# A two-layer hybrid trunk: three rounded passes for every mixer chunk, with half slots, a ring of six and remainders on GpSimd

## Chip, cores and metric

The kernel runs on one core of one Trainium2 chip. The metric is the device time of one launch in microseconds, from the first to the last instruction and what lies around them; lower is better. Engines: TensorE (PE) multiplies, VectorE (DVE), ScalarE (ACT) and GpSimd (POOL) work on tiles in SBUF, and SyncE (SP) issues the DMA of the weights.

## The reference

The input x is 256 tokens by 1024 channels, f32. There are two layers. In each:

- `h = rmsnorm(x)`, then one projection `z = h @ w_in` whose columns feed four mixers and four gates. A is a gated MLP (`u * (W_s @ layernorm(v))`), B is causal pooling with windows 2, 4, 8 and 16, C is RWKV-7 (eight heads of 64, a delta-rule state), D is Mamba-2 SSD (eight heads, a causal convolution of width 4).
- `merged = sum_k sigmoid(G_k) * (y_k @ w_branch[k])`, then `x = x + merged @ w_out`.
- `h = rmsnorm(x)`, then a dense SwiGLU (inner width 3584) in layer 0, and the best two of eight SwiGLU experts for each token in layer 1.

A last rmsnorm gives the output. Mixer C normalises `kk` by the norm of each head, and its output by the variance of each head; both are sums over 64 channels.

## The kernel before

**The stream of weights.** All large weights lie in HBM as one stream of chunks of 128 x 2048 f32 (1 MB), in the order of use: 19 chunks of the projection (NZ; `Z_UNITS` names them zg, xbc, v, u, b, c), 24 of the merge (N_MERGE: for each of 8 steps two of gates and one of a branch projection), 4 of the output, 42 of a feed-forward block, and so on; 472 in all. SP loads them into `ring`, seven slots, and reuses a slot when PE has raised `chunks_used`.

**Two kinds of matmul.** For a plain f32 matmul PE reads `ring` and `h` directly (two records in the trace for each call of `mm`). For a rounded product, `three` makes three passes: rounded weight by rounded activation, rounded by remainder, and remainder by rounded. ACT rounds the whole chunk into `w_high` (two slots, L1167 in the mixer), and DVE subtracts it from the chunk in place, which gives `ring_low` (`z_low`, L1660). Before the change this is done for the first NS = 12 chunks of a layer's mixer, for the dense FFN and for the experts; chunks 12 to 18, the merge and the output are plain f32.

**The order of work.** PE's order is written out by hand. `project` computes a layer's chunks 0 to 18; between them stand `mixer_d_rows` (after chunk 13), `mixer_d_out` (after 15), `mixer_d_norm` (after 16) and `mixer_a`, `mixer_b` (after 17). Then comes `mixer_c`, a long serial chain: LoRA matmuls, head norms, then for each of two chunks of time the scores and six levels of doubling, in which PE, DVE and ACT hand tiles to each other. Between its links PE does quarters of merge chunks as filler. `SIDE` lists how many: 12 before the LoRA matmuls ("cw"), 4 before the head sums ("ss"), 12 before the bonus ("bo"), 8 before the transposes ("kt"), one to three at each level, 4 each at "mu" and "va". The branches are merged in the order A, B, D, C, so C is needed last. `merge` does the remaining chunks and the output matmuls.

**Each engine works in program order.** ACT evacuates the projection's banks (`evacuate`), takes the sigmoids of the gates (`gates`, L1158) and the exponentials and roots of the mixers. DVE does the rest of the mixers and multiplies gates by projections (`products`). POOL makes the pooling of mixer B and adds the products of steps 2 to 7 into `mg` (L1330). For head norms PE sums the 64 channels of each head with a 128 x 128 matrix of ones and zeros, `heads`, so that the sums are spread over all channels, and DVE takes the reciprocal of 128 x 1024 numbers (L1546 for `kk`, L1618 for the output).

**Lines that the text below uses.** L1006 and L1009 are the squares and the square root of a norm on ACT; between them ACT rounds the first two chunks (`meanwhile`). L1051 is an exponential of a 128 x 1024 tile on ACT. L1492 and L1494 are mixer C's token shift on DVE: one difference of 128 x 3584 and 14 multiply-adds. L1555 makes `nb`, the last tile that PE's transposes "kt" and "nt" (L466) wait for. L1570 masks a tile out of PSUM, and L1572 adds the identity to it in SBUF. L1594 adds a level's result.

Of the kernel before, what the change touches and what calls it, by code (L numbers as in the profile page):

```python
# [28 lines left out]
RING = 7  # L48
# [9 lines left out]
NS = 12  # L58
MERGE_ORDER = [0, 1, 3, 2]
# [5 lines left out]
SIDE = [("cw", 12), ("ss", 4), ("bo", 12), ("kt", 8)]  # L65
# [4 lines left out]
SIDE += [("mu", 4), ("va", 4)]  # L70
# [16 lines left out]
for _name, _k in PP_LIST:  # L87
# [6 lines left out]
           ("off", LEVELS * P), ("count", 4 * T), ("reset", 4 * T), ("sel", H * P), ("slots", CAP), ("slot", 1)]  # L94
# [4 lines left out]
NCC = _n  # L99

SW_LIST = [("w_s", 512), ("pool", 512), ("w2a2", 512), ("g2", 512), ("dt", 64), ("router", 64)]
SW, _n = {}, 0
for _name, _k in SW_LIST:
# [11 lines left out]
for _c in range(NCH):  # L115
    _r = 2 * _c
# [9 lines left out]
    if _c == 0:  # L126
        M_USES += [("S", 2)]
M_USES += [("mu0", 1), ("mu1", 2), ("va0", 3), ("va1", 0)]
# [30 lines left out]
def trunk(nc, x_in, stream, pp_in, cc_in, sw_in, rep_in, out):  # L159
    with ExitStack() as ctx:  # L160
# [6 lines left out]
        x = sb("x", [P, DT, T])  # L167
        h = sb("h", [P, DT, T])
        ring_at = -(-nc.sbuf_base // 32) * 32
        ring = sb("ring", [P, RING, CW])  # L170
        cc = sb("cc", [P, NCC])
        pp = sb("pp", [P, L, NPP])
        sw = sb("sw", [P, NSW])
        rep = sb("rep", [P, NREP])
        rstd = sb("rstd", [P, T])
        rms = sb("rms", [P, T])
        small = sb("small", [P, 256])
        arena_at = -(-nc.sbuf_base // 32) * 32
        arena = sb("arena", [P, 28264])
# [68 lines left out]
        wb = area(24168, 512)  # L248
        ub = area(24680, 512)
# [5 lines left out]
        oo = tiles(12840, 4)  # L255
# [3 lines left out]
        k2 = tiles(24168, 4)  # L259
# [3 lines left out]
        sg = area(25192, 1024).rearrange("p (b f) -> p b f", b=2)  # L263
        mg = tiles(26216, DT)

        def sg_of(step, i):
# [5 lines left out]
        gbanks = [0, 1, 2, 3, 0, 1, 2]  # L272
        gu = tiles(4096, FT)
        sil = tiles(11264, RING)
# [3 lines left out]
        h_high = part("h_high", 0, [DT, T])  # L278
        h_low = part("h_low", 2048, [DT, T])
        gu_high = part("gu_high", 4096, [FT, T])  # L280
        gu_low = part("gu_low", 15976, [FT, T])
        w_high = part("w_high", 23144, [2, CW])
# [36 lines left out]
        low_ready = sem("low_ready")  # L319
        v_seq = sem("v_seq")  # L320
# [10 lines left out]
            "hg_filled hg_high_ready hg_ready silu_tok hid_ready hid_turned eu_high_ready eu_ready y_ready zeroed back_filled back_drained h_split h_split_high gu_part").split()}  # L331
# [45 lines left out]

        class Count:
# [17 lines left out]
        def _(sp):  # L396
# [5 lines left out]
            for s in range(RING):  # L402
                sp.dma_start(ring[:, s, :], stream[s]).then_inc(landed[s], 16)
                if s == 1:
                    sp.dma_start(sw[:, :], sw_in[0]).then_inc(layer_in, 16)
                    sp.dma_start(cc[:, first:NCC], cc_in[:, first:NCC]).then_inc(all_consts_in, 16)
                    sp.dma_start(rep[:, :], rep_in[0]).then_inc(layer_in, 16)
# [21 lines left out]
        def _(pe):  # L429
# [31 lines left out]

            def turn(l, stage, parts):
# [5 lines left out]

            def project(l, lo, hi):

                for n in range(lo, hi):
                    name, i = Z_UNITS[n]
                    slot = (chunk0(l) + n) % RING
                    if n < NS:

                        pe.wait_ge(low_ready, l * (NS + N_FFN) + n + 1)
                        low = ring_low[:, slot, :].rearrange("p (b m) -> p b m", b=BLK)
                        high = w_high[:, n % 2, :].rearrange("p (b m) -> p b m", b=BLK)
                    else:
                        w = chunk(chunk0(l) + n)  # L480
                    if name == "v":

                        if i == 0:
                            g_free(pe, l, ("v", 0))
                            g_free(pe, l, ("v", 1))
                        wl = ring_low[:, slot, :].rearrange("p (k f) -> p k f", k=4)
                        wh = w_high[:, n % 2, :].rearrange("p (k f) -> p k f", k=4)

                        for c in range(NCH):
                            for k in range(4):  # L490
                                tc = slice(c * P, (c + 1) * P)
                                last = three(gb(("v", c))[:, :], h_high[:, 4 * i + k, tc], h_low[:, 4 * i + k, tc],
                                             wh[:, k, :], wl[:, k, :], i == 0 and k == 0, i == 1 and k == 3)
                    else:
                        g_free(pe, l, (name, i))
                        for j in range(2):
                            for k in range(DT):
                                if n == 0 and j == 0 and k % 2 == 0:

                                    pe.wait_ge(S["h_split"], 8 * l + k // 2 + 1)  # L500
                                o = gb((name, i))[:, j * T:(j + 1) * T]
                                if n < NS:
                                    last = three(o, high[:, DT * j + k, :], low[:, DT * j + k, :], h_high[:, k, :], h_low[:, k, :],
                                                 k == 0, k == DT - 1)
# [213 lines left out]
            def merge_quarters(l, lo, hi):  # L718

                for n in range(lo, hi):  # L720
# [28 lines left out]
                    if part == 3:  # L749
                        last.then_inc(chunks_used, 1)  # L750
# [1225 lines left out]
```

## Time and profile before

| | |
|---|---|
| median of 3 runs | 2349.38 us (2345.57 to 2350.28) |
| the profiled execution | 2349.66 us, span 2347.6 us |
| PE busy | 2235.1 us, 95% of the span |
| DVE busy | 1433.7 us, 61% |
| ACT busy | 1052.7 us, 45% |
| POOL busy | 51.6 us, 2% |
| DMA | 504.66 MB, mean 215 GB/s |
| TensorE clock granted | 0.96 of full |

"Busy" is the time in which an engine executes an instruction, not the time in which it is needed. The profile's views are: groups of instructions by line; windows, which give each engine's busy time in a stretch; waits; the chain of work that ended last, in order of time; and the timeline. Times in the views are counted from the start of the span.

### The profile page before, as it was taken

The page shows a single profiled execution, that of the slowest core. Times are in us where ns is not written, and L with a number is a line of the kernel's source. Part 1 is how long each engine was busy: PE and PEld are TensorE (multiplying, and loading weights), DVE is VectorE, ACT ScalarE, POOL GpSimd, SP SyncE. Part 2 cuts the span into 40 slices and gives each one's busy share as a digit, 9 for nine tenths or more (in the row PEclk, how much of TensorE's full clock was granted, in tenths as well). Part 3 has the DMA queues.
Part 4 walks back from the last instruction along what each step waited for, and adds up shares of the span by engine and source line. Part 5 has one row for each costly group of instructions (what it writes and reads, how often), then busy time and mean ns, then how long its engine had stood idle before and what let it go on. Part 6 is the DMA issues. An engine that isn't in the chain of part 4 may idle for free.

```text
span 2347.6 us, 30978 instructions
## 1 busy us (share of the span) xinstructions
PE 2235.1 (95%) x12088; PEld 1825.8 (78%) x12088; DVE 1433.7 (61%) x1395; ACT 1052.7 (45%) x886; POOL 51.6 (2%) x52
## 2 busy tenths in 40 slices
PE   7979999989999897999998899999999999999997
PEld 6868889879999786888977677777777777777775
DVE  3544643235553453554222788888888888888885
ACT  4312211123333432211111577777777767777673
POOL 0100000000000010000010000000000000000000
PEclk9979999989999998999898899999999999999999
DMA  7422212325455342321131498989999999989892
GB/s 299 173 72 108 90 55 72 141 108 180 179 179 182 123 144 72 128 76 67 54 126 72 181 368 330 365 341 356 349 347 349 349 347 348 368 329 367 330 367 108
DMA packets 69342, 504.66 MB, mean 215 GB/s; under 512 B 7696, under 2 KB 7952, under 8 KB 8208
## 3 DMA queue, kind: packets, MB, share of 16 engines
q1 hardware_dynamic: 68832, 500.57, 56.9%
q10 hardware_dynamic: 432, 2.95, 0.3%
q8 instruction: 61, 1.00, 0.2%
q14 instruction: 17, 0.14, 0.0%
HBM read 502.44 MB, written 1.05 MB: 214 GB/s over the span
## 4 chain that ended last, share of the span: by engine, by line
PE 93%; DVE 3%; ACT 1%; issue 1%; DMA 0%; SPq 0%; DVEq 0%; ACTq 0%
PE g L433 61%; PE m L433 30%; PE m L466 1%; PE m L903 1%; DVE h L1354 1%; DMA ring<-stream 0%; DVE arena L1572 0%; DVE rstd L1352 0%; DVE arena L1570 0%; ACT w_high L1167 0%; ACT arena L1006 0%; ACT L1009 0%; DVE h L1871 0%; DVE arena L1432 0%; DVE arena L1428 0%
## 5 line engine op out<-in xcount | busy, mean ns | idle before, releaser
L1750 DVE TENSOR_TENSOR ring_low<-ring,we_high 128x2048 fp32r<-128x2048 f32 x336 | 769.1, 2290 | 153.3 <-ACT we_high L1212 152.9
L1212 ACT ACTIVATE we_high<-ring 128x2048 fp32r<-128x2048 f32 x336 | 644.2, 1918 | 273.8 <-PE g L433 180.9
L433 PE MATMUL g<-we_high,hg_high 128*96 128x512 f32 x896 | 358.4, 400 | 10.3 <-DVE ring_low L1750 10.3
L433 PE MATMUL g<-ring_low,hg_high 128*96 128x512 f32 x896 | 353.8, 395 | 0.0
L433 PE MATMUL g<-we_high,hg_low 128*96 128x512 f32 x896 | 352.6, 394 | 0.0
L433 PE MATMUL g<-h,ring 128*128 128x256 f32 x1472 | 338.2, 387 | 0.0
L433 PEld LDWEIGHTS g<-h,ring 128*128 128x128 f32 x1472 | 282.3, 194 | 42.2 <-issue 4.3
L433 PE MATMUL m<-arena 128*128 128x128 f32 (+7 forms) x1832 | 264.7, 309 | 20.1 <-DVE arena L1428 9.4
L433 PEld LDWEIGHTS m<-arena 128*128 128x128 f32 (+3 forms) x1832 | 235.6, 195 | 47.2 <-issue 14.7
L433 PE MATMUL g<-h_high,w_high 128*128 128x256 f32 x768 | 220.3, 287 | 27.0 <-DVE h_low L1667 25.1
L433 PE MATMUL g<-h_low,w_high 128*128 128x256 f32 x768 | 219.0, 285 | 0.0
L433 PE MATMUL g<-h_high,ring_low 128*128 128x256 f32 x768 | 218.7, 285 | 0.0
L433 PEld LDWEIGHTS g<-we_high,hg_high 128*96 128x96 f32 x896 | 145.0, 162 | 70.8 <-DVE ring_low L1750 11.0
L433 PEld LDWEIGHTS g<-we_high,hg_low 128*96 128x96 f32 x896 | 144.6, 161 | 62.8
L433 PEld LDWEIGHTS g<-ring_low,hg_high 128*96 128x96 f32 x896 | 144.7, 162 | 59.1
L433 PE MATMUL g<-arena,ring 128*128 128x256 f32 x768 | 180.3, 394 | 7.5 <-issue 7.5
L433 PE MATMUL m<-we_high,eu_high 128*96 128x512 f32 x448 | 177.3, 396 | 0.0
L433 PE MATMUL m<-we_high,eu_low 128*96 128x512 f32 x448 | 176.4, 394 | 0.0
L433 PE MATMUL m<-ring_low,eu_high 128*96 128x512 f32 x448 | 176.3, 393 | 0.0
L433 PEld LDWEIGHTS g<-arena,ring 128*128 128x128 f32 x768 | 150.4, 198 | 29.6 <-issue 8.3
L433 PEld LDWEIGHTS g<-h_high,w_high 128*128 128x128 f32 x768 | 147.1, 191 | 29.3 <-issue 29.2
L433 PEld LDWEIGHTS g<-h_low,w_high 128*128 128x128 f32 x768 | 147.8, 192 | 0.1
(240 smaller groups left out, 2224.4 us busy)
## 6 DMA issues: line engine op xcount, KB each, us to landing
ring<-stream SPq DMA_DIRECT2D x472, 1024.0 KB, 4.8
cc<-cc_in SPq DMA_DIRECT2D x1, 2352.5 KB, 16.4
sw<-sw_in SPq DMA_DIRECT2D x1, 1088.0 KB, 11.2
sw<-sw_in ACTq DMA_DIRECT2D x1, 1088.0 KB, 6.2
x<-x_in SPq DMA_DIRECT2D x1, 1024.0 KB, 4.8
out<-h ACTq DMA_DIRECT2D x1, 1024.0 KB, 3.9
rep<-rep_in SPq DMA_DIRECT2D x1, 768.0 KB, 17.8
rep<-rep_in ACTq DMA_DIRECT2D x1, 768.0 KB, 7.7
```

The costliest lines, as they stand in the source:

```text
L433: return pe.matmul(o, a, b, start=start, stop=stop, skip_group_check=True)
L466: last = pe.transpose(mb(stage)[:, i * P:(i + 1) * P], src, ident)
L903: last = pe.transpose(mbank[g % 2][:, j * CAP:(j + 1) * CAP], hid_tok[:, g % 2, j * P:(j + 1) * P], ident[0:CAP, 0:CAP])
L1212: A(we_high[n % 3][:, :], ring[:, slot, :], ACT.Copy).then_inc(high_ready, 1)
L1354: q.add(V.scalar_tensor_tensor(h[:, k, :], x[:, k, :], gain(k), rstd[:, :], ALU.mult, ALU.mult), done)
L1750: TT(ring_low[:, slot, :], ring[:, slot, :], we_high[n % 3][:, :], ALU.subtract).then_inc(low_ready, 1)
```

## The change

- **All mixer chunks in three passes.** `NS` no longer decides; chunks 12 to 18, the merge and the output are rounded too, and so are the projection of `dt` (moved from after chunk 1 to after chunk 4), `h`, the branch outputs (`y_high`, `y_low`) and the merged tiles (`mg_high`, `mg_low`).
- **Half slots.** ACT rounds halves of 128 x 1024 into five slots (`z_w`, N_SLOTS). `z_highs` issues them in ACT's program order, before and after each evacuation and at each filler quarter; half n waits until PE has used half n - 5. At the start of a layer's norm five halves are rounded, where two chunks were.
- **Remainders.** DVE subtracts for chunks 0 to 7 (`z_low`), POOL for chunks 8 to 46 (`lows`), in halves. POOL also makes the remainders of the branch outputs A, B and D (`y_lows`, at fixed places in its sequence) and its sums for steps 2 to 5; DVE makes the sums of steps 6 and 7 and the remainders of C's output and of `mg`.
- **Ring of six slots**, for the whole kernel. The dense FFN's loops of 14 are written out, and its PSUM banks rotate by four.
- **Reciprocals per head.** `by_head` sums a head's channels into 8 rows; ACT takes the root and DVE the reciprocal of 8 x 256, and a second group of matmuls (`over_heads`, "sr" and "vr") spreads them over the channels, where DVE multiplies them in.
- **Fillers.** "kt" goes from 8 to 4 quarters, "sr" and "vr" get 4 each.
- **Constants.** The tables count, reset and sel (3072 of 4705 columns) are no longer kept in SBUF; POOL makes the reset mask, and 16 columns of count are loaded alone.

```diff
-RING = 7
+RING = 6
+N_SLOTS = 5
+HALF = 1024
+N_DVE = 8
-SIDE = [("cw", 12), ("ss", 4), ("bo", 12), ("kt", 8)]
+SIDE = [("cw", 12), ("ss", 4), ("bo", 12), ("sr", 4), ("kt", 4)]
...
-SIDE += [("mu", 4), ("va", 4)]
+SIDE += [("mu", 4), ("va", 4), ("vr", 4)]
...
+        def half_free(eng, l, n, b):
+
+            at = 2 * (l * N_MIX + n) + b - N_SLOTS
+            if at >= 0:
+                before, m, half = at // (2 * N_MIX), at % (2 * N_MIX) // 2, at % 2
+                if half:
+                    eng.wait_ge(chunks_used, chunk0(before) + m + 1)
+                else:
+                    eng.wait_ge(half_used, before * N_MIX + m + 1)
...
+                    n = Z_UNITS.index(unit)
+                    z_highs(l, 2 * n + 1 + N_SLOTS)
                     act.wait_ge(chunks_used, unit_chunk(l, unit) + 1)
...
                     q.add(ins, g_drained[G_PLAN[unit][0]])
+                    z_highs(l, 2 * n + 2 + N_SLOTS)
...
+                act.wait_ge(S["ya_ready"], NCH * (l + 1))
+                y_split(l, 0)
                 side("cw")
...
+                for q4 in range(lo, hi):
+                    (step, i), part = MERGE_CHUNKS[q4 // 4], q4 % 4
+                    z_highs(l, 2 * NZ + q4 // 2 + N_SLOTS)
+                    if (step, i) == (6, 2) and part == 0:
+                        y_split(l, 2)
...
+                    if (step, i) == (2, 0):
+                        m_done(act, l, "b0")
+                        m_done(act, l, "b1")
+                        act.wait_ge(a_seq, q.n[id(a_seq)])
+                        y_split(l, 1)
...
                 norm(lambda i: act.wait_ge(ffn_drained, FT + i + 1) if l else None, lambda: filled(act, l, "norm1"),
-                     lambda ins: drain(l, "norm1", ins), lambda: (z_high(l, 0), z_high(l, 1)))
+                     lambda ins: drain(l, "norm1", ins), lambda: z_highs(l, N_SLOTS))
...
+                gates(l, SIDE_END, 12 * STEPS)
+                z_highs(l, 2 * (NZ + N_MERGE) + N_SLOTS)
+                for i in range(4):
+                    act.wait_ge(merged, 2 * STEPS * l + 13 + i)
+                    A(mg_high[:, 2 * i:2 * i + 2, :], mg[i], ACT.Copy).then_inc(S["mg_high_ready"], 1)
+                z_highs(l, 2 * N_MIX)
...
+            def lows(l, lo, hi):
+
+                for n in range(lo, hi):
+                    for b in range(2):
+                        if (n, b) == (NZ + 1, 1):
+                            y_lows(l, 0)
+                        if (n, b) == (NZ + 8, 0):
+                            y_lows(l, 1)
+                        if (n, b) == (NZ + 14, 1):
+                            y_lows(l, 3)
+                        pool.wait_ge(z_high_ready, 2 * (l * N_MIX + n) + b + 1)
+                        G.tensor_tensor(half_ring(ring_low, l, n, b), half_ring(ring, l, n, b), half_slot(l, n, b), ALU.subtract)\
+                            .then_inc(pool_low_ready, 1)
+                        m = n - NZ - 3
+                        if b == 0 and 0 <= m < N_MERGE and MERGE_CHUNKS[m][1] == 2 and 2 <= MERGE_CHUNKS[m][0] < 6:
+                            adds(l, MERGE_CHUNKS[m][0])
...
-                q.step(V.reciprocal(tmp1[:, :, :], tmp1[:, :, :]))
-                q.step(TT(kk[:, :, :], kk[:, :, :], tmp1[:, :, :], ALU.mult))
+                q.step(V.reciprocal(rstd[0:H, :], rstd[0:H, :]), S["sr_ready"])
...
-                va = tiles(8720, 4)
-                q.step(V.reciprocal(va[:, :, :], va[:, :, :]))
-                q.step(TT(oo[:, :, :], oo[:, :, :], va[:, :, :], ALU.mult))
+                q.step(V.reciprocal(rstd[0:H, :], rstd[0:H, :]), S["vr_ready"])
+                side("mu", "vr")
```

## Rows read from the trace of the kernel before

**Rows 1.** Windows: us, busy time of each engine, granted clock, DMA share, GB/s

```profile
177.50:205.20 27.70, 27.70 (x129) 24.13 (x127) 10.67 (x19) 4.72 (x9) 0.00 (x0) 1.00 0.31 114
205.20:258.60 53.40, 51.77 (x250) 44.96 (x249) 30.26 (x40) 18.21 (x27) 0.00 (x0) 1.00 0.33 118
...
1405.50:1531.50 126.00, 126.00 (x581) 90.00 (x581) 106.93 (x66) 90.83 (x63) 0.00 (x0) 1.00 0.91 349
```

**Rows 2.** The chain that ended last, in order of time: start us, us, what

```profile
169.24 2.89 issue
...
442.17 27.63 PE g L433 x128
469.79 3.77 issue
473.56 30.73 PE g L433 x128
...
515.27 83.08 PE g L433 x672
598.35 1.97 issue
600.32 80.87 PE g L433 x672
...
763.92 3.69 ACT w_high L1167 x2
```

**Rows 3.** Timeline before the transposes "kt": start us, us, engine line op out<-in

```profile
251.13 1.23 DVE L1555 TENSOR_TENSOR arena<-arena 128x1024 f32<-128x1024 f32 x1
...
257.63 1.04 PE L466 MATMUL m<-cc,arena 128*128 128x128 f32 x8
```

**Rows 4.** Groups by line and shape, POOL and ACT: busy us, mean ns

```profile
L1324 POOL TENSOR_TENSOR arena<-arena 128x1024 f32<-128x1024 f32 x2 | 4.7, 2350 | 0.2
...
L1051 ACT ACTIVATE arena<-arena 128x1024 f32<-128x1024 f32 x2 | 2.1, 1056 | 2.4 <-DVE arena L1435 2.3
```

**Rows 5.** Timeline inside a level of mixer C

```profile
280.27 0.69 DVE L1594 TENSOR_TENSOR arena<-m,arena 128x512 f32<-128x512 f32 x1 [0.20 <-PE m L433]
...
281.80 1.04 PE L466 MATMUL m<-cc,arena 128*128 128x128 f32 x8
```

**Rows 6.** Timeline where POOL and DVE work at once

```profile
258.84 2.68 POOL L1330 TENSOR_TENSOR arena<-arena 128x512 f32<-128x512 f32 x2 [151.12 <-DVE small L1342]
259.79 0.69 DVE L1570 TENSOR_TENSOR arena<-m,cc 128x512 f32<-128x512 f32 x1 [0.27 <-PE m L433]
260.51 1.55 DVE L1572 TENSOR_TENSOR arena<-arena,cc 128x512 f32<-128x512 f32 x1
```

**Rows 7.** Groups by line and shape, DVE, first 510 us: busy us, mean ns

```profile
L1494 DVE SCALAR_TENSOR_TENSOR arena<-arena,pp 128x256 f32<-128x256 f32 x14 | 5.6, 477 | 0.0
...
L1492 DVE TENSOR_TENSOR arena<-arena 128x3584 f32<-128x3584 f32 x1 | 3.9, 3893 | 8.0 <-ACT arena L1028 8.0
```

**Rows 8.** Timeline, SP's issues at the start

```profile
3.84 0.43 SPq L406 DMA_DIRECT2D cc<-cc_in  x1
4.31 0.49 SPq L407 DMA_DIRECT2D rep<-rep_in  x1
```

**Rows 9.** The page's DMA issues: number, KB each, us from issue to landing

```profile
ring<-stream SPq DMA_DIRECT2D x472, 1024.0 KB, 4.8
cc<-cc_in SPq DMA_DIRECT2D x1, 2352.5 KB, 16.4
...
rep<-rep_in SPq DMA_DIRECT2D x1, 768.0 KB, 17.8
```

**Rows 10.** The chain at the start: table load and square root on ACT

```profile
13.91 1.28 ACT L1009
15.19 0.01 issue
15.20 0.48 ACT rms L1009
```

**Rows 11.** Waits of SP's queue in one expert: us in total, times, longest

```profile
SPq L413 <- PE g L433: 66.4, 28, 4.0
```

More of the change, by code:

```diff
@@ L472, in project @@
                     name, i = Z_UNITS[n]
[L473 to L496, printed above, removed]
-                            for k in range(DT):
[L498 to L504, printed above, removed]
-                                else:
-                                    last = mm(o, w[:, DT * j + k, :], h[:, k, :], k == 0, k == DT - 1)
@@ L721, in merge_quarters @@
                     (step, unit), part = MERGE_CHUNKS[n // 4], n % 4
-                    w = chunk(chunk0(l) + NZ + n // 4)
+                    half, quarter = part // 2, part % 2
+                    wh, wl = halves(l, NZ + n // 4, half)
                     if unit < 2:
@@ L726, in merge_quarters @@
                             g_free(pe, l, ("gate", step, unit))
-                        j = part // 2
-                        for k in range(4 * (part % 2), 4 * (part % 2) + 4):
-                            last = mm(gb(("gate", step, unit))[:, j * T:(j + 1) * T], w[:, DT * j + k, :], h[:, k, :],
-                                      k == 0, k == DT - 1)
+                        for k in range(4 * quarter, 4 * quarter + 4):
+                            last = three(gb(("gate", step, unit))[:, half * T:(half + 1) * T], wh[:, quarter, k % 4, :], wl[:, quarter, k % 4, :],
+                                         h_high[:, k, :], h_low[:, k, :], k == 0, k == DT - 1)
                     else:
@@ L1148, in gates @@
+                side("vr")
             def gates(l, lo, hi):
[L1150 to L1158 removed]
@@ L1169, in split_h, with y_split @@
+            highs = [0]
+            def y_split(l, branch):
+                for i in range(2):
+                    if branch == 2:
+                        act.wait_ge(S["yc_ready"], 2 * l + i + 1)
+                    two = slice(2 * i, 2 * i + 2)
+                    A(y_high[:, two, :], (yA, yB, yC, yD)[branch][:, two, :], ACT.Copy).then_inc(S["y_high_ready"], 1)
             def split_h(n):
@@ L1656, in z_low @@
             def z_low(l, n):
[L1658 to L1660 removed]
+                for b in range(2):
+                    dve.wait_ge(z_high_ready, 2 * (l * N_MIX + n) + b + 1)
+                    TT(half_ring(ring_low, l, n, b), half_ring(ring, l, n, b), half_slot(l, n, b), ALU.subtract).then_inc(z_low_ready, 1)
             def split_h(n):
```

424 lines of the change are left out of this document (271 added, 153 removed), and 4 rows, old and new, of the table M_USES.

## The prediction, made before the changed kernel was run

> **What bounds the kernel now.** I read the page first. It gives TensorE as busy for nearly the whole span (the share stands in the table above). So I asked for the same thing by stages, and for the chain of work in order of time, to see where that share means "nothing else matters" and where it hides waits.
>
> The expert stage is eight passes of 126.0 us, in which PE never idles, at full granted clock [rows 1]. The change leaves its instructions alone, except that the ring has six slots, not seven. The dense FFN is three-pass matmuls with one gap, 1.97 us between its two loops of fourteen chunks [rows 2]. What the change can move is the mixer: up to the dense FFN's first matmul at 515.27 in layer 0, and as much again in layer 1, nearly 1,000 us.
>
> In the mixer PE is nearly full in the fillers of mixer C (the first two stretches of [rows 1]), but elsewhere it waits, named "issue": 2.89 us at 169.24 for the normalised v, 3.77 at 469.79 for the last merged tiles [rows 2]. The reader is to see two more things in the chain. The price of a chunk in each form: four f32 chunks (128 records) take 27.63 us, 6.91 each; fourteen rounded three-pass chunks (672 records) take 80.87 us, 5.78 each. And the price of a wait beyond itself: the same fourteen chunks take 83.08 us when they follow a wait, 2.2 more; four f32 chunks then take 30.73, 3.1 more [rows 2]. I call this the restart price.
>
> **What the change saves.** 35 chunks a layer (7 of the projection, 24 of gates and branches, 4 of the output) go from 6.91 to 5.78: 1.13 us each, 0.28 a quarter, 39.6 a layer. That is the whole direct gain: 79 us, 3.4%. Two matmul groups are added to each layer, sr and vr, each about the 1.9 us of the groups that they resemble. The two wide reciprocals go, and I give that nothing: the first one's result reached PE's turn with time to spare (the last operation of that chain ends at 252.36, PE uses it after 257.63) [rows 3], and the filler work covers the other.
>
> **What feeds the three passes.** Each half chunk now needs a rounding on ACT and a remainder on GpSimd. ACT's copy of 128x1024 is 1.06 us; GpSimd's subtract of that size is 2.35 [rows 4]. PE uses a half in 2.89 us, so GpSimd keeps up, alone, with 0.5 us to spare. Five slots mean that a remainder is made four halves, 11.6 us, ahead. In the levels of mixer C the filler is 0.28 us shorter; DVE's last result there ends at 280.96 and PE takes it at 281.80 [rows 5], so that slack holds, and DVE reads PSUM there.
>
> **The lock.** GpSimd would be busy for 78 x 2.35 = 183 us of each mixer, where it is now nearly idle. The one place where it works beside DVE on SBUF data shows the price: GpSimd's two adds run from 258.84 to 261.52; DVE's L1572, with two SBUF operands, starts at 260.51 and takes 1.55 us, ending 0.54 after GpSimd. L1570, a tile of the same size that comes from PSUM, takes 0.69 under the same adds [rows 6]. So such an operation waits for the GpSimd instruction to end: up to 2.35 us with the new one. The Trainium skill, "SBUF — State Buffer", section "Who interferes with whom", says that a DVE instruction with two SBUF inputs and a GpSimd instruction that reads SBUF exclude each other for a whole instruction, and that issue order decides who blocks. The trace agrees for DVE (1.55 against 0.69); it shows no GpSimd instruction kept waiting. By the rule the sum is the one below; if DVE alone waited, step 3 would be the +9 given there.
>
> The trace does not show who gets in when both are queued. I bound it: DVE keeps a run of independent operations together and GpSimd waits for the run (short waits in all), or one GpSimd instruction slips in ahead of each DVE operation (long waits). Mixer C's early work is mostly such runs, so I take values nearer to the first. From below the bound is no waiting at all, a rival below.
>
> **The working, for one layer** (minus is faster):
> 1. Chunks 0 to 13: two converted, -2.3. The remainders of chunks 8 to 13 run against the convolution's multiply-adds, which have slack: 0.
> 2. Chunks 14 to 17 and mixer D's ends: three of the chunks save 3.4. The fourth's saving is lost to a longer wait for the normalised v, whose chain starts earlier. A half rounding (1.06) now stands on ACT ahead of the decay's exponential and of yD's square, both awaited by PE: +2.1. The product xde meets one GpSimd remainder: +1; the two normalisations of v, each with two multiply-adds of SBUF operands, meet two: +4. Sum +3.7.
> 3. Chunk 18 to the LoRA matmuls, 27.7 us before [rows 1]. Here POOL must make branch A's remainders (two of 1.34 us, as the pair of adds in [rows 6]) before that of the fourth half after chunk 18, and DVE starts its token-shift work at the same moment: 3.89 us, then fourteen of 0.48 [rows 7], all with two SBUF inputs. With DVE's run first: the difference runs from 6.9 to 10.8 us after the start of chunk 18, one remainder of A to 12.1, the run (5.6 together) to 17.8, the other remainder to 19.1, GpSimd's half to 21.5. PE wants it at 5.8 + 3 x 2.9 = 14.5: 7 us, less 4.5 saved by four chunks, plus a restart of 2.2: +4.6. Alternating, the LoRA inputs are 11 us late: +9. I take +6.
> 4. From there to the transposes of ka and nb, 53.4 us before [rows 1]: 24 quarters save 6.8, sr costs 2. The exponentials stand behind a gate, a rounding and branch B's split on ACT, and three DVE operations of 1.23, with two SBUF inputs, and the two products from PSUM must follow the sr matmuls inside one filler chunk of 5.8. That just fits; each GpSimd remainder they meet adds up to 2.35, so 3 to 8 late; with 5.3 and a restart of 2.2, +2.7 in all.
> 5. Masks and scores, ten DVE operations with two SBUF inputs per chunk of time: +2.
> 6. Levels to the last branch chunk: 60 quarters would save 16.9; I count 15. vr costs 2. Then a new wait: after vr only one chunk, not two, stands before branch C's projection, and ACT must do a sigmoid (about 0.8 with its start) and a half rounding (1.06) behind it; GpSimd takes up that half's remainder (2.35) before DVE can make yC's two (0.69 each): 5.6 in all, and a restart of 2.2. Sum -5.
> 7. Output, 3.77 + 30.73 before [rows 2]. ACT rounds mg only after the last branch chunk, behind another half (1.06), whose remainder (2.35) is again ahead of DVE's first (0.69): with the start PE waits 4.4, then restarts (2.2) and needs 4 x 5.78 = 23.1: -4.8.
>
> Sum: -2.3 + 3.7 + 6 + 2.7 + 2 - 5 - 4.8 = +2.3, for two layers +4.6.
>
> **The starts.** ACT's norm now rounds five halves ahead of the square root, and the fifth is in chunk 2. Chunk 2 is issued behind the constants and rep. Those land at 20.2 and 22.1 us (issued at 3.84 and 4.31 [rows 8], landed 16.4 and 17.8 later [rows 9]); rep's 0.79 MB take the 1.9 us between, 0.41 MB/us. With 0.84 MB of constants in place of 2.41, rep lands 3.8 us earlier, at 18.3, and chunk 2, another 1.05 MB and some short packets later, near 21.5. Then 1.06 for the half, 1.28 for the table and 0.48 for the root, which ends at about 24.4 us, where it ended at 15.68 [rows 10]: +8.7, once. In layer 1 the data are there and five halves take 5.3 us against 3.69 [rows 2]: +1.6. Unrolling the dense loop takes away its wait of 1.97 at 598.35 [rows 2]: -2.0.
>
> The total is 4.6 + 8.7 + 1.6 - 2.0 = +12.9. The profiled execution took 2349.66 us (span 2347.6), 0.3 above the median of 2349.38, so I predict 2362.
>
> **The ring.** A transfer lands 4.8 us after its issue [rows 9], and SP waited 66.4 us of an expert's 126 for PE to free a slot in the up projection alone [rows 11]. With six slots, three chunks of 126 / 42 = 3.0 us pass between a slot's release and ACT's turn on it, 9.0 us, so about 4 us are left: 0.
>
> **Rivals.**
> - Slower by rounding, locks and the start (my forecast), 0.55: about 2362, its own range 2345 to 2385.
> - Faster, 0.28: the lock rarely bites, because DVE's SBUF work falls into GpSimd's gaps. Then steps 2 to 5 are about -2, -2.5, -5 and 0, step 6 -8 and the others stay near: -25 a layer, -50, and with the starts -42: 2308. For it: average load is low (DVE is busy 10.67 of 27.7 us, and 30.26 of 53.4 [rows 1]). Against it: in exactly those stretches GpSimd needs 2.35 of each 2.89. It decides when all lock delays are under about 4 us a layer.
> - Strict alternation, 0.12: +9 in step 3, +8 in 4, +5 in 5, more in 2 and 6: +20 a layer, +48: 2398.
> - The six-slot ring makes the experts late, 0.05: 0.1 us on each of 336 chunks is +34. Against it: the 4 us above.
>
> Within 0.2%, 4.7 us, about what a measurement here can tell from nothing, I put 0.10, from between the first two. Faster gets 0.30, slower 0.60. The range is 2310 to 2397: down to the rival without locks, up to alternation.
>
> **What would show it.** In the changed profile: the first square root near 24 us, not 15.7 (the start); the projection's later chunks at 5.78; DVE multiply-adds of 0.48 stretched to two or more us wherever POOL is busy, L1494's counterpart above all; PE waiting for POOL's remainder in the fillers ahead of LoRA, for the ab chain at the ka transposes, and for yC's and mg's remainders; experts still 126.0. I am wrong if DVE's operations keep their lengths beside GpSimd, if the square root of the first norm still ends before 17 us, or if SP's six slots show in the expert period.

## The result, and the profile of the changed kernel

The changed kernel takes **2366.5 us** (median of 4 runs, 2364.6 to 2370.1) where the kernel before takes 2347.5 (4 runs beside it): ratio 1.0082, 95% interval 1.0063 to 1.0101. It is 19.0 us slower; the forecast was 2362, and +12.9. Its profiled execution took 2370.1, span 2368.2, 20.6 more than the span of before.

Windows of the changed kernel: chunk 18 to the LoRA matmuls, from there to the first level's "n" products, and one expert (columns as in [rows 1]):

```profile
186.33:220.04 33.71, 22.97 (x192) 22.57 (x191) 27.09 (x18) 12.77 (x17) 22.78 (x9) 0.89 0.35 125
220.04:282.26 62.22, 55.14 (x353) 49.83 (x353) 33.73 (x41) 30.66 (x41) 32.77 (x14) 0.84 0.23 85
...
1424.97:1550.97 126.00, 126.00 (x582) 90.10 (x581) 106.93 (x66) 90.83 (x63) 0.00 (x0) 1.00 0.92 350
```

Against the two layer-0 stretches of [rows 1], VectorE does almost the same work in the first and is busy 27.1 us where it was busy 10.7. PE idles 10.7 us of the first and 7.1 of the second, and its clock falls with that: 0.89 and 0.84, where it was 1.00 in both. The expert still takes 126.0.

Some groups of the changed kernel, of both layers together (busy us, mean ns of one):

```profile
L1420 POOL TENSOR_TENSOR ring_low<-ring,z_w 128x1024 fp32r<-128x1024 f32 x156 | 382.1, 2468 | 483.9 <-ACT z_w L1224 483.7
L1502 DVE SCALAR_TENSOR_TENSOR arena<-arena,pp 128x256 f32<-128x256 f32 x48 | 67.0, 1466 | 0.2
L1619 DVE SCALAR_TENSOR_TENSOR arena<-arena,pp 128x256 f32<-128x256 f32 x28 | 44.8, 1673 | 0.1
L1399 POOL TENSOR_TENSOR y_low<-arena,y_high 128x512 fp32r<-128x512 f32 x12 | 20.4, 1719 | 48.0 <-ACT y_high L1241 48.0
L1669 DVE TENSOR_TENSOR arena<-arena 128x1024 f32<-128x1024 f32 x2 | 6.9, 3431 | 16.5 <-ACT small L1151 16.5
L1670 DVE TENSOR_TENSOR arena<-arena 128x1024 f32<-128x1024 f32 x2 | 6.7, 3366 | 0.0
L1591 DVE TENSOR_SCALAR arena<-arena,small 128x512 f32<-128x512 f32 x4 | 6.0, 1501 | 0.1
```

The token shift's multiply-adds (L1619), 477 ns each in [rows 7], take 1673 ns; the products of 128x1024, 1.23 us in [rows 3], take 3.4: their own time and nearly one GpSimd half (2.47). GpSimd's halves are near their free length (2.35 in [rows 4]).

The chain that ended last, through mixer C of layer 0 (start us, us, what):

```profile
192.88 3.90 DVE arena L1617
...
196.80 22.44 DVE arena L1619 x14
...
220.04 9.36 PE m L463 x24
```

This is the prediction's step 3: fourteen operations that took 5.6 us take 22.4, and PE waits 9.3 us for them. The timeline shows how; here are three pieces of it:

```profile
201.84 2.56 POOL L1420 TENSOR_TENSOR ring_low<-ring,z_w 128x1024 fp32r<-128x1024 f32 x1
202.08 2.61 DVE L1619 SCALAR_TENSOR_TENSOR arena<-arena,pp 128x256 f32<-128x256 f32 x1
...
204.37 2.59 POOL L1420 TENSOR_TENSOR ring_low<-ring,z_w 128x1024 fp32r<-128x1024 f32 x1
204.61 2.63 DVE L1619 SCALAR_TENSOR_TENSOR arena<-arena,pp 128x256 f32<-128x256 f32 x1
...
218.76 0.47 DVE L1619 SCALAR_TENSOR_TENSOR arena<-arena,pp 128x256 f32<-128x256 f32 x1
```

One VectorE operation and one GpSimd half take strict turns of 2.5 us; each VectorE operation starts 0.24 us after a half has started and ends 0.3 after that half's end. It goes on while GpSimd has halves. After the seventh, at 217.0, it has none, since PE, waiting, frees no slot, and the last five operations take 0.47 us each again. The last line of the chain is a second price: the 24 LoRA products take 9.36 us. In the chain of the kernel before they take 4.82:

```profile
205.30 4.82 PE m L433 x24
```

The granted clock is 1.00 there. In the changed kernel it falls to 0.50 in PE's wait and stays there through the products (windows, columns as in [rows 1]):

```profile
216.00:220.00 4.00, 0.00 (x0) 0.00 (x0) 3.96 (x9) 0.73 (x2) 0.97 (x1) 0.50 0.00 0
220.00:224.00 4.00, 3.96 (x13) 3.40 (x14) 2.03 (x6) 0.98 (x3) 0.00 (x0) 0.50 0.00 0
224.00:228.00 4.00, 4.00 (x10) 2.71 (x10) 3.13 (x3) 2.53 (x7) 0.00 (x0) 0.50 0.00 0
```

The spans divide as follows (us). A part ends where PE starts the next one: the dense part, layer 1, and the first product behind the choice of experts ("experts" is all from there to the end of the span):

| | PE starts | mixer 0 | dense, norm | mixer 1 | experts |
|---|---|---|---|---|---|
| before | 21.6 | 493.7 | 260.1 | 507.9 | 1064.3 |
| changed | 30.0 | 500.9 | 254.6 | 516.5 | 1066.1 |
| difference | +8.4 | +7.3 | -5.5 | +8.6 | +1.8 |

### The profile page after: what moved, and what is told of

The parts are those of the page before. It is cut to its first block, busy times and chain, and to the rows that moved or that the text cites. A ratio compares the mean times of both kernels' runs of the same rounds, so it can differ in the third digit from the quotient of the medians.

```text
span 2368.2 us, 33655 instructions
## 1 busy us (share of the span) xinstructions
PE 2180.4 (92%) x13256; PEld 1828.5 (77%) x13256; DVE 1557.2 (66%) x1428; ACT 1204.1 (51%) x1073; POOL 450.9 (19%) x222
## 3 DMA queue, kind: packets, MB, share of 16 engines
q8 instruction: 75, 1.23, 0.2%
## 4 chain that ended last, share of the span: by engine, by line
PE 86%; DVE 7%; ACT 2%; POOL 2%; issue 2%; DMA 1%; SPq 0%; DVEq 0%; ACTq 0%; POOLq 0%
PE g L463 54%; PE m L463 30%; DVE arena L1619 2%; PE m L507 1%; PE m L944 1%; POOL ring_low L1420 1%; DMA ring<-stream 1%; DVE h L1474 1%; ACT z_w L1224 1%; DVE arena L1696 0%; DVE arena L1617 0%; DVE rstd L1472 0%; POOL arena L1444 0%; DVE arena L1593 0%; DVE arena L1670 0%
## 5 line engine op out<-in xcount | busy, mean ns | idle before, releaser
L1420 POOL TENSOR_TENSOR ring_low<-ring,z_w 128x1024 fp32r<-128x1024 f32 x156 | 382.1, 2468 | 483.9 <-ACT z_w L1224 483.7
L463 PE MATMUL g<-h_high,ring_low 128*128 128x256 f32 x1504 | 429.3, 285 | 0.0
L463 PE MATMUL g<-h_high,z_w 128*128 128x256 f32 x1056 | 311.6, 295 | 31.9 <-DVE h_low L1808 27.1
L1224 ACT ACTIVATE z_w<-ring 128x1024 fp32r<-128x1024 f32 x188 | 196.2, 1054 | 255.6 <-PE g L463 247.6
L463 PE MATMUL g<-h_low,z_w 128*128 128x256 f32 x1056 | 302.1, 286 | 0.0
L463 PE MATMUL m<-arena 128*128 128x128 f32 (+7 forms) x1832 | 271.8, 315 | 28.3 <-issue 13.4
L463 PEld LDWEIGHTS g<-h_high,ring_low 128*128 128x128 f32 x1504 | 290.3, 193 | 0.0
L463 PEld LDWEIGHTS g<-h_high,z_w 128*128 128x128 f32 x1056 | 206.4, 195 | 40.8 <-issue 33.7
L463 PEld LDWEIGHTS g<-h_low,z_w 128*128 128x128 f32 x1056 | 206.2, 195 | 0.4
L1814 DVE TENSOR_TENSOR ring_low<-ring,w_high 128x2048 fp32r<-128x2048 f32 x42 | 96.2, 2291 | 56.7 <-ACT w_high L1253 56.7
```

The source lines that it names most:

```text
L463: return pe.matmul(o, a, b, start=start, stop=stop, skip_group_check=True)
L1224: A(half_slot(l, n, b), half_ring(ring, l, n, b), ACT.Copy).then_inc(z_high_ready, 1)
L1420: G.tensor_tensor(half_ring(ring_low, l, n, b), half_ring(ring, l, n, b), half_slot(l, n, b), ALU.subtract)\
L1814: TT(ring_low[:, slot, :], ring[:, slot, :], w_high[:, n % 2, :], ALU.subtract).then_inc(low_ready, 1)
```

## The experiments

The theory under test: the loss is that GpSimd's remainders and VectorE's operations on SBUF keep each other out ("the lock"), plus the five halves ahead of the first root. Its rivals are in the expectations.

**One, four halves ahead of the root.**

```diff
-                     lambda ins: drain(l, "norm1", ins), lambda: z_highs(l, N_SLOTS))
+                     lambda ins: drain(l, "norm1", ins), lambda: z_highs(l, 4))
```

> The changed kernel, with four instead of five halves split by ScalarE ahead of the norm's root. Theory: the root ended 8.4 us late (24.09 for 15.68) because the fifth half, the first of chunk 2, waited for a transfer that landed at 21.24. Then the root ends at about 15.7 again, PE starts at about 22, and the whole is 7 to 8.4 us shorter than the changed kernel (about 2358 us); layer 1, where the ring is full, does not change. Rival: the constants that the norm needs land late by themselves, and the time stays at 2366.

Measured: 2358.3 us, 8.2 under the changed kernel, inside the 7 to 8.4 of the theory. PE starts at 21.1 for 30.0.

**Two, GpSimd at work, but not on two tensors.**

```diff
-                return half_slot(l, n, b), half_ring(ring_low, l, n, b)
+                return half_slot(l, n, b), half_ring(ring_low, l, n, b) if n < N_DVE else half_slot(l, n, b)
...
-                        G.tensor_tensor(half_ring(ring_low, l, n, b), half_ring(ring, l, n, b), half_slot(l, n, b), ALU.subtract)\
-                            .then_inc(pool_low_ready, 1)
...
+                        for i in range(15):
+                            q.step(G.memset(small[:, 192:256], 0.0))
+                        G.memset(small[:, 192:256], 0.0).then_inc(pool_low_ready, 1)
```

> The changed kernel, in which GpSimd's subtraction of each half is replaced by 16 fillings of a 64-column scrap, chained, which keep it at about the same pace (16 of some 0.15 us, 2.4 us), and PE reads the rounded half once more in place of the remainder, so the remainder of chunks 8 on is left out of the result. Theory (a GpSimd operation of two tensors and a VectorE one keep each other out for their whole length): the 14 token-shift operations go back from 22.4 to about 5.7 us, the convolution from 34.2 to about 10, and some 12 to 18 us of each layer go, 24 to 36 in all, to 2330 to 2342 us. Rival (the chunks wait for GpSimd's pace and for ScalarE's order, whatever GpSimd does to the memory): VectorE's groups fall, but the time stays within 6 us of 2366. Second rival (both engines only share the bandwidth of the memory, so that any traffic of GpSimd slows VectorE): the groups stay long.

Measured: **2310.1 us**, 56.4 under the changed kernel and 1.7% under before (ratio 0.9833, 0.9819 to 0.9848). The convolution and the token shift, groups of this kernel (line numbers 4 higher), and one of the two products:

```profile
L1506 DVE SCALAR_TENSOR_TENSOR arena<-arena,pp 128x256 f32<-128x256 f32 x48 | 19.6, 479 | 0.2
L1623 DVE SCALAR_TENSOR_TENSOR arena<-arena,pp 128x256 f32<-128x256 f32 x28 | 15.2, 614 | 0.1
...
L1673 DVE TENSOR_TENSOR arena<-arena 128x1024 f32<-128x1024 f32 x2 | 2.5, 1226 | 16.6 <-ACT small L1151 16.6
```

The convolution is back at 479 ns and the product at 1226. The token shift keeps 614, for branch A's two remainders (y_low) are still subtractions on GpSimd. GpSimd was busy as long as in the changed kernel (449.7 us for 450.9), and with the gaps in its chain a half took it some 3.3 us, more than the subtraction; at the end of the convolution PE even waited longer for it (chunk 14 at 132.1 for 123.7). The 16 fillings write as many columns as the subtraction, 1024, and read none. So it is neither GpSimd's load nor its lateness that costs, but that its instructions read the tensors: both rivals fall. The size was underestimated, 56 for 24 to 36. Layer 0, changed kernel to this one: to chunk 14 +8.8, chunks 14 to 18 -4.4, to the LoRA matmuls -6.9, to the "n" products -9.8, from there to the last branch chunk -11.6, and the rest -1.6. Without the late chunk 14, 34 us of a layer hang on GpSimd's reading, a third of them in masks, scores, levels and yC's stall, for which the theory had hardly allowed.

**Three, fourteen operations made two.**

```diff
-                for j in range(CT):
-                    ins = V.scalar_tensor_tensor(zc[:, j, 1:T + 1], dif[:, j, :], par(l, "mix", j), zc[:, j, 1:T + 1], ALU.mult, ALU.add)
-                    (q.add(ins, v_seq) if j < CT - 1 else q.step(ins, S["zc_mixed"]))
+                mix = pp[:, l, PP["mix"]:PP["mix"] + CT]
+                q.step(TT(dif[:, :, :], dif[:, :, :], along(mix, T), ALU.mult))
+                q.step(TT(now, dif[:, :, :], now, ALU.add), S["zc_mixed"])
```

> The changed kernel, with the 14 token-shift multiply-adds of 128x256 replaced by one product and one sum over 128x3584. Theory (whole operations alternate): the price is per operation, so two long ones meet at most two GpSimd halves: 2 x 3.9 us and up to 2 x 2.45, 8 to 13 us in place of 22.4, and 9 to 14 us less in each layer as far as nothing else is late there (GpSimd's halves in turn wait up to 3.9 us); the sum 10 to 25 us, to 2341 to 2356. Rival (a shared bandwidth: an operation beside GpSimd takes 4 times its time however long it is): the two take 25 us or more, and the kernel gets slower by 5 to 15 us.

Measured: 2352.1 us, 14.4 less. In VectorE's timeline below, the difference takes 3.89 us as before and the two new operations 4.87 and 4.84, in place of 22.4. Their sum is within the 8 to 13 us of the theory and not the rival's 25 or more: the price is at most one GpSimd instruction per VectorE operation, whatever its length. But the lock turned round. GpSimd's timeline of this kernel:

```profile
191.95 8.61 POOL L1399 TENSOR_TENSOR y_low<-arena,y_high 128x512 fp32r<-128x512 f32 x2 [14.90 <-ACT y_high L1241]
200.52 20.25 POOL L1420 TENSOR_TENSOR ring_low<-ring,z_w 128x1024 fp32r<-128x1024 f32 x7
```

and VectorE's:

```profile
190.63 3.89 DVE L1617 TENSOR_TENSOR arena<-arena 128x3584 f32<-128x3584 f32 x1 [7.75 <-ACT arena L1071]
...
194.56 4.87 DVE L1619 TENSOR_TENSOR arena<-arena,pp 128x3584 f32<-128x3584 f32 x1
199.47 4.84 DVE L1620 TENSOR_TENSOR arena<-arena 128x3584 f32<-128x3584 f32 x1
204.34 9.52 DVE L1625 TENSOR_SCALAR arena<-arena,pp 128x256 f32<-128x256 f32 x4
```

Branch A's two remainders, of a size that takes 1.28 us alone (the median of the changed kernel's twelve), take 8.61 together, and GpSimd's first half behind them 5.99 alone: each ran out against a long VectorE operation. The four products by `k_k` (L1625), which met no half in the changed kernel (1.1 us together), now take turns with GpSimd and need 9.52, but PE doesn't wait for them. PE now waits 8.3 us in one place, for GpSimd's half, where it had waited 9.3 for VectorE, and from chunk 18 to the LoRA matmuls it takes 33.2 us, 33.7 in the changed kernel. Of layer 0's 12.2 us, 4.5 are seen behind that: the wait now ends at 206.6, chunk matmuls follow it, and the 24 LoRA products, with the clock up again, take 4.82 us for 9.36. The rest of the 12.2 has no single place; PE's mean granted clock over the mixer is 0.91, for 0.89 in the changed kernel. Layer 1 gives 6.5.

**Four, the remainders of chunks 8 to 11 back to VectorE.**

```diff
-N_DVE = 8
+N_DVE = 12
...
                 for k in range(4):
+                    z_low(l, 8 + k)
```

> The changed kernel, with the remainders of chunks 8 to 11 given back to VectorE, between the four rows of the convolution, as before the change. Theory (alternation): the 24 multiply-adds of the convolution, 34.2 us in the changed kernel, fall to 12 to 16, and VectorE pays 8 halves of 1.1 us; GpSimd reaches pooling some 10 us earlier, so its remainders of chunks 12 and on are there when PE wants them: 3 to 5 us less in each layer, to about 2358. Rival: PE's own rate ends these chunks, the cover holds, and the time stays within 2 us of 2366.

Measured: 2366.0 us, 0.5 under the changed kernel, which is no difference: the rival was right. The 48 multiply-adds fell from 67.0 to 40.2 us (mean 908 ns), and nothing came of it: GpSimd's pooling, not the convolution, is on the chain there, and it ended only 1.2 us earlier. A lock in a place with slack costs nothing.

**Five, the kernel before with a ring of six and the dense part written out.** ScalarE's and VectorE's loops are written out in the same way.

```diff
-RING = 7
+RING = 6
...
-                with pe.Fori(0, FT // (2 * RING)) as i:
-                    for s in range(2 * RING):
+                for s in range(FT):
...
-                                last = three(gbank[gbanks[s % RING]][:, j * T:(j + 1) * T], high[s % 2][:, DT * j + k, :],
+                            last = three(gbank[s % 4][:, j * T:(j + 1) * T], high[s % 2][:, DT * j + k, :],
```

> The kernel before, with only its ring cut from seven slots to six and the dense feed-forward part written out as the change has it. Theory: the writing out gives the 6.6 us that the dense part got shorter (245.6 to 239.0), and the ring of six costs 0 to 2: about 2341 to 2343 us. Rival: the dense part got shorter through something else of the change, and this kernel takes what the one before takes, or longer by what the smaller ring costs.

Measured: 2341.9 us, ratio 0.9973 (0.9964 to 0.9982), 5.6 under before, the total that the theory gives. Its profile bears out less: the dense part is 2.4 us shorter (243.2 for 245.6; the seam was 1.97), and the experts' part is that of before (1064.0 for 1064.3), so the ring of six costs nothing. Mixer 1, which this edit touches only by the ring, is 5.3 shorter in this profile. Its windows (before, then this kernel, columns as in [rows 1]) point to the clock:

```profile
775.35:1283.25 507.90, 478.01 (x2679) 421.69 (x2679) 207.36 (x351) 104.42 (x143) 25.45 (x21) 0.93 0.28 98
...
773.43:1276.05 502.62, 472.83 (x2679) 418.00 (x2679) 207.15 (x351) 104.41 (x143) 25.45 (x21) 0.94 0.27 99
```

PE idles as long (29.9 and 29.8 us), and the same 2679 instructions take it 5.2 us less. Whether that belongs to the edit is not shown: single executions of before lie 5.8 us apart themselves (2344.8 to 2350.6). The total does belong to the edit, for this kernel's eleven times all lie below them (2337.3 to 2342.9), but some 3 of its 5.6 us have no place that the profile shows.

**Six, the kernel before with its reciprocals per head.** The other engines' side of it is that of the change.

```diff
-                two_banks(l, "ss", lambda j: heads, lambda j: tmp1[:, j, :])
+                head_sums(l, "ss", tmp1)
...
+                side("sr")
+                over_heads(l, "sr")
...
-                two_banks(l, "va", lambda j: heads, lambda j: tiles(7696, 4)[:, j, :])
+                head_sums(l, "va", tiles(7696, 4))
+                side("vr")
+                over_heads(l, "vr")
```

> The kernel before, with only its reciprocals per head (sums over the heads, a reciprocal of 8 rows, a spreading product). Theory, by the prediction's prices: two more groups of spreading products per layer, of some 1.9 us each, and the steps between the engines hidden, so 4 to 8 us more in all, to 2351 to 2355. Rival: the shorter reciprocals give more than that back on VectorE where it ends the wait, and the time is the same or 2 to 5 us less.

Measured: 2356.1 us, ratio 1.004 (1.0026 to 1.0054), +8.6. The prediction's price was 2 for each of four groups, 8 in all. The profile does not show the place: it was taken of the shortest run (2351.1; the other four 2355.5 to 2356.2), with mixer 0 0.6 us shorter and mixer 1 3.0 longer than in before.

**Seven, GpSimd's pooling two chunks later.**

```diff
-                lows(l, N_DVE, NS + 2)
+                lows(l, N_DVE, NS + 4)
```

> The changed kernel, in which GpSimd makes the remainders of chunks 14 and 15 before its pooling for branch B, not behind it. Theory: in the changed kernel chunk 14's first remainder (2.35 us, from 121.27) stood behind 13.8 us of pooling and PE resumed at 123.67; PE's records show it idle for 2.2 of the 20 us ahead of that, so 2 to 3 us of each layer go, and the pooling moves into the stretch where PE waits for mixer D anyway: 3 to 6 us in all, to 2360 to 2363. Rival: the convolution, which ends on VectorE at 111.6, and the pooling's own users (the last of branch B, the token shift) become late by what is gained: within 2 us of 2366, or slower.

Measured: 2371.6 us, 5.1 more, where 3 to 6 less were expected. Chunk 14 started 1.8 us earlier, as the theory had it. But of mixer D's four products L1550 of each layer, 0.69 us each in the changed kernel without exception, two got longer. The chain that ended last has them with 2.5 and 2.7 us in layer 0 (start us, us, what), and chunk 18 started 3.0 us later than in the changed kernel:

```profile
141.28 2.54 DVE arena L1550
...
143.85 2.73 DVE arena L1550
```

What they met was not the pooling, which was over by 133.4, but the remainders that the pooling had put off. GpSimd's timeline, the changed kernel and this one:

```profile
121.27 21.06 POOL L1420 TENSOR_TENSOR ring_low<-ring,z_w 128x1024 fp32r<-128x1024 f32 x9
...
133.51 12.51 POOL L1420 TENSOR_TENSOR ring_low<-ring,z_w 128x1024 fp32r<-128x1024 f32 x5
```

In the changed kernel the run of remainders behind the pooling ends at 142.3, just before L1550 starts at 143.1; here it lasts to 146.0, and L1550 starts at 141.3. That the changed kernel's order is free of this is luck of position. The pooling's own operations take turns as well, for the last two multiply-adds of the changed kernel's convolution, beside L1439 and L1440, take 2.21 and 1.75 us for 0.48, but there VectorE has slack. "Moves into the stretch where PE waits for mixer D anyway" was wrong, for what PE waits for there is VectorE, and GpSimd holds VectorE up.

**Eight, two swaps on ScalarE.**

```diff
-                    z_highs(l, 2 * NZ + q4 // 2 + N_SLOTS)
                     if (step, i) == (6, 2) and part == 0:
                         y_split(l, 2)
+                    z_highs(l, 2 * NZ + q4 // 2 + N_SLOTS)
...
-                z_highs(l, 2 * (NZ + N_MERGE) + N_SLOTS)
                 for i in range(4):
```

> The changed kernel, with two swaps on ScalarE: it splits branch C's output before it rounds the next half chunk, and the merged result before the half chunk that follows the last branch chunk. Theory: each of these stalls (PE waited 5.6 and 4.3 us in the changed kernel) holds one rounding of 1.06 and one GpSimd remainder, for which VectorE's own remainder waited (up to 2.35 less 0.69): 2.5 to 3.4 us off each of four stalls, 10 to 14 in all, to 2353 to 2357. Rival: what comes last there is the chain of VectorE and PE before ScalarE's turn, and the swaps only make the next half late: within 2 us of 2366.

Measured: 2353.8 us, 12.7 less. Around branch C's projection, the changed kernel (engine timelines):

```profile
473.11 2.67 POOL L1420 TENSOR_TENSOR ring_low<-ring,z_w 128x1024 fp32r<-128x1024 f32 x1 [0.69 <-ACT z_w L1224]
...
473.66 3.26 DVE L1760 TENSOR_TENSOR y_low<-arena,y_high 128x512 fp32r<-128x512 f32 x2
```

and with the swaps:

```profile
474.14 1.29 DVE L1759 TENSOR_TENSOR y_low<-arena,y_high 128x512 fp32r<-128x512 f32 x2
...
475.73 2.38 POOL L1419 TENSOR_TENSOR ring_low<-ring,z_w 128x1024 fp32r<-128x1024 f32 x1 [2.84 <-ACT z_w L1224]
```

VectorE's two remainders take 1.29 us in place of 3.26, because no GpSimd half is ahead of them. PE's gap falls from 5.6 to 3.6 us here and from 4.3 to 1.6 at the merged result: 4.7 in layer 0, a little under the 5 to 6.8 that I gave two stalls. The PE runs behind the two gaps are shorter too, by 1.0 and 1.5 us: the clock again (in the first 3.4 us behind the second gap it is 1.00 here and 0.63 in the changed kernel). Nor is the first mg remainder free, 2.52 us for 0.68: another half still meets it.

**Nine and ten, the edits together.** Nine has edits one, three, seven and eight, ten has one, three and eight.

> The changed kernel with four edits together: four halves ahead of the root, the token shift as two operations, the pooling two chunks later, the two swaps on ScalarE. If they work on separate waits, their sum: -8.2 and -14.4 as measured, -3 to -6 and -10 to -14 as expected of the other two: 36 to 43 us less, 2324 to 2331, and 16 to 24 below the kernel before. Rival: the gains share waits (the token shift and GpSimd's queue above all), and about half of the last two is left: 2335.

> The changed kernel with three of the four edits (four halves, token shift as two operations, the two swaps), the pooling left where the change has it. Theory: the three work on separate waits, and what the late pooling cost by itself (+5.1) was in the version with all four: 2366.5 - 8.2 - 14.4 - 12.7 = 2331. Rival: with the other edits in place the late pooling costs nothing or helps, and this is 2334 or more.

Measured: nine 2334.2 us, ten **2327.2** (ratio to before 0.9909, 0.9894 to 0.9924). Nine lands on its rival's 2335, but not by shared waits: without the late pooling the three others add up, 8.2 + 14.4 + 12.7 = 35.3 expected and 39.3 found (where the 4.0 beyond the sum come from is not traced). The late pooling costs 7.0 here, 5.1 alone, so ten's rival falls. Ten is faster than both kernels.

**Eleven: ten with 16 more operations of 128x256 made 5 of 128x1024.** For instance

```diff
-                for j in range(4):
-                    ins = V.tensor_scalar(kk[:, j, :], k[:, j, :], par(l, "k_k", j), None, ALU.mult)
-                    (q.add(ins, v_seq) if j < 3 else q.step(ins, S["kr_ready"]))
+                four_of = lambda name: along(pp[:, l, PP[name]:PP[name] + 4], T)
+                q.step(TT(kk[:, :, :], k, four_of("k_k"), ALU.mult), S["kr_ready"])
```

> The version with three edits, and in mixer C three more sets of per-block VectorE operations (4 products for k_k, 8 for k_a, 4 for r_k, each 128x256) made as 1, 2 and 2 operations over 128x1024. Theory (each operation beside GpSimd can cost a GpSimd half, 2.45 us): the 4 products at k_k alone took 5.6 us in the changed kernel for 1.4 without GpSimd; together some 4 to 8 us of VectorE per layer are saved, of which the chain to the exponentials lets through 1 to 4: 2 to 8 in all, to 2323 to 2329. Rival: longer operations keep GpSimd's halves waiting and PE waits for those: within 2 us of the version with three, or slower.

Measured: 2329.2 us; the ratios to before, 0.9911 and 0.9909, can't be told apart. The rival's outcome, but not for the rival's reason. The products by `k_k` fell from 9.5 to 3.2 us a layer, and PE's two waits around them are the same in both kernels, 8.3 us before the LoRA matmuls and 5.4 before "sr": nothing that PE waits for hangs on them. The expectation's premise was wrong as well: in the changed kernel these four products took 1.1 us together, not 5.6, and in ten no half meets the operations of `k_a` and `r_k` (346 to 467 ns each).

## Why the prediction came out as it did

The direction and the mechanism were right; the time came out 4.5 us above the forecast, and that nearness is partly luck. It hides two larger errors of opposite sign: the two mixers cost 15.9 us more where 4.6 were forecast, and the dense part 6.6 less where 2.0 were. Also, the kernel before measured 1.9 us less beside the changed one than the 2349.4 from which the forecast started. Layer 0 by the prediction's steps, measured between the same points of the two chains:

| step | predicted | measured |
|---|---|---|
| 1, chunks 0 to 13 | -2.3 | -4.3 |
| 2, chunks 14 to 17 | +3.7 | +4.7 |
| 3, chunk 18 to LoRA | +6 | +6.0 |
| 4, LoRA to the "n" products | +2.7 | **+8.8** |
| 5, masks and scores (measured: the first chunk of time) | +2 | +1.4 |
| 6, from there to the last branch chunk | -5 | -3.8 |
| 7, output | -4.8 | -5.6 |
| sum of a layer | +2.3 | +7.3 |
| first start; layer 1's start | +8.7; +1.6 | +8.4; +1.2 |
| dense part | -2.0 | **-6.6** |

- **The start** is right: root at 24.1 (24.4 forecast), and experiment one takes the whole of it away with one half.
- **The lock** is the mechanism: without GpSimd's subtractions of halves the kernel runs 56 us faster. That this kernel's 2310 us are near the 2308 of the lock-free rival is partly luck, for in it chunk 14 comes 8.8 us later in each layer, which the rival does not have, and the dense part gives 4.6 us more than forecast. What the three passes give and the waits take shows in mixer 0 alone: PE's busy time there falls from 466.1 us to 439.9, at a mean granted clock of 0.89 for 0.94, and its idle time rises from 27.6 to 61.0.
- **Step 3 agrees by luck.** The +6 lay between two orders, VectorE's run first (+4.6) and strict turns (+9), and each of these holds a restart of 2.2 us. The restart falls behind the LoRA wait, so by the points of the table it is measured in step 4, and the +6.0 is to be set against 3.8. Where both engines had a queue they took strict turns, the order that I had given 0.12: PE waits 1.4 and 9.3 us in this stretch, 10.7 in all, and alternation was to make the LoRA inputs 11 us late. For the whole kernel (2398 us) strict turns overstated it, because they end when GpSimd runs out of halves.
- **Steps 3 and 4 together are the term that was mis-sized**: 14.8 us for 8.7. Some 2.4 of that are the longer wait in step 3. In step 4 the wait before "sr" was right (5.4 for 5.3; the pair of 128x1024 products takes 3.4 us each for 1.23). The restarts were not: the forecast has 2.2 each, 4.4. Behind the LoRA wait the clock was at 0.50 and the LoRA products took 9.36 us for 4.82, so 4.5. Behind the "sr" wait it was at 0.50 again, the eight products took 3.75 us for some 1.9 and the chunk behind them 7.8 for 5.7, together 3.9.
- **Step 5** covers both chunks of time in the forecast. The second one's masks and scores cost 2.4 us more and are measured in step 6; together they are +3.8 for +2.
- **The stalls of yC and mg** were forecast as 5.6 and 4.4 and measured as 5.6 and 4.3. That a half stands ahead of them, rounded on ScalarE and subtracted on GpSimd, is shown by experiment eight; 3.6 and 1.6 us of the two gaps stay when it is moved away.
- **Pooling and the convolution:** "slack, 0" for the convolution was right, and experiment four shows it; it is GpSimd's own pooling that ends that stretch.
- **The heads:** 8 forecast, +8.6 measured by itself (6 to 13 by its interval).
- **The dense part** gave 6.6 in place of 2.0. The seam of 1.97 is 2.0 of it. In addition the 1344 products of the up projection take 159.8 us, in before 163.9 without the seam (83.1 and 80.9), and in experiment five, with the same written-out code, 163.5. So those 4 us are not the writing out. About one lies in the first 20 us, where the mean clock was 0.93 and in the others 0.87 and 0.89. Behind them it is 1.00 in all three, and still PE does 8.5 products a us in the changed kernel and 8.3 in the others. What makes them some 2% faster stays open; the two kernels also differ in where `h_high`, `h_low` and `w_high` lie in SBUF, which no run tests.
- **The ring of six** costs nothing, by the experts' 126.0 and by experiment five. The 1.8 us of the experts' part are in all versions of the changed kernel (1.5 to 1.9) and not in experiment five; I have no cause for them.

The Trainium skill's page "SBUF — State Buffer", "Who interferes with whom", has exclusion for whole instructions, both ways. The traces agree in both directions, of which the trace of before could show only one: VectorE's 128x1024 products go from 1.23 to 3.4 us, and in experiment three GpSimd's two 128x512 remainders from 1.28 to 4.3 on average.

## What to carry to other kernels

Moving element-wise work to an idle GpSimd is not free, however idle it is: count each VectorE operation on SBUF in the same stretch as longer by up to one GpSimd instruction, and each GpSimd one by a VectorE operation, and then look only at those that PE waits for. Cheap cures are to make many short VectorE operations few where PE waits for them (14.4 us here; where it doesn't, experiment eleven, nothing), and to keep the next half's rounding behind the split that PE waits for, so that GpSimd stays quiet (12.7 us). Putting GpSimd work off can push its bulk onto VectorE operations that had been free of it (experiment seven, 5.1 us lost). A wait of 4 to 9 us on PE has to be charged with its length and with the slow clock behind it, 1 to 4.5 us here.

## What the runs showed that I had not expected

- VectorE operations with one SBUF tensor and a per-partition scalar are kept waiting as well: L1591, 128x512, takes 545 ns at best and 1501 in the mean; L1647, 128x256, is 0.35 us without GpSimd and up to 2.58; L1625 goes from 0.35 to 2.4 in experiment three.
- GpSimd's fillings (16 of 64 columns, 154 ns each) do not disturb VectorE at all: its convolution stays at 479 ns.
- Between two full queues the turns are strict, one instruction each (202 to 217 us above), and a VectorE operation of 3.9 or 4.9 us holds GpSimd off just as well: a half of 2.4 us took 5.99.
- The same products at the same granted clock differ by 2% between two versions (8.5 and 8.3 a us, behind the first 20 us of the up projection).
- The same 2679 instructions of mixer 1 with the same idle time took PE 478.0 and 472.8 us in two kernels, at a mean granted clock of 0.93 and 0.94.
